# Mixture of experts: gate and up products in one PSUM bank, the down product behind the next expert's first products

## What is computed

```python
for e in range(N_EXPERTS):                       # 16; two of them count for each row
    he = jax.nn.silu(h2 @ w_gate[e]) * (h2 @ w_up[e])          # 1024 -> 256
    moe = moe + combine[..., e:e + 1] * (he @ w_down[e])       # 256 -> 1024
x = x + moe
y = rmsnorm(x, g_final)
```

## Time and profile before

| | before |
|---|---|
| median of 3 runs (lowest to highest) | 462.22 us (460.56 to 463.78) |
| profiled execution: its time, its span | 466.0 us, 464.2 us |
| PE busy | 431.6 us, 93% of the span |
| DVE, ACT, POOL busy | 229.3, 150.2, 108.9 us |
| chain that ended last | PE 78%, DVE 8%, ACT 4%, issue 3%, DMA 2%, POOL 2% |
| two of its lines | gate and up (L1120) 25%, down (L1128) 12% |
| DMA queues: q1 (SP), q0 (POOL) | 71.97 MB, 18.96 MB |

### The profile page before, as it was taken

How to read it: one execution, slowest core, us unless ns; L and a number is a source line. 1 busy time by engine, 2 the same in 40 slices (tenths; PEclk the granted TensorE clock), 3 DMA queues, 4 the chain that set the end, 5 groups by cost and what they waited for, 6 DMA issues and landing times.

```text
span 464.2 us, 7463 instructions
## 1 busy us (share of the span) xinstructions
PE 431.6 (93%) x2858; PEld 351.0 (76%) x2858; DVE 229.3 (49%) x590; ACT 150.2 (32%) x397; POOL 108.9 (23%) x200
## 2 busy tenths in 40 slices
PE   7899999999999998999987899999999999999970
PEld 3786999988867766888763888888877777778850
DVE  3854233536688985443338462222455555544441
ACT  5474223425567663321113210112222211222240
POOL 2011002000342341310003022222443333333221
PEclk9999999999999999999999999999999999999995
DMA  7851607124000299132215999998999988952110
GB/s 269 286 151 48 214 1 229 55 74 118 1 3 0 95 419 388 75 140 91 92 56 209 367 368 363 342 356 343 341 353 340 325 322 327 339 185 61 50 59 20
DMA packets 32072, 91.38 MB, mean 197 GB/s; under 512 B 11193, under 2 KB 11705, under 8 KB 27942
## 3 DMA queue, kind: packets, MB, share of 16 engines
q1 hardware_dynamic: 20790, 71.97, 42.2%
q0 software_dynamic: 11248, 18.96, 11.5%
HBM read 86.38 MB, written 26.01 MB: 242 GB/s over the span
## 4 chain that ended last, share of the span: by engine, by line
PE 78%; DVE 8%; ACT 4%; issue 3%; DMA 2%; POOL 2%; POOLq 0%; SPq 0%; DVEq 0%; ACTq 0%
PE ps L1120 25%; PE ps L1128 12%; PE ps L774 10%; PE ps L776 9%; PE ps L775 9%; PE ps L1070 2%; PE ps L1113 2%; PE ps L895 2%; PE ps L930 2%; DMA region_x<-in_x_prompt 1%; PE ps L913 1%; PE ps L1057 1%; DMA region_x<-h_rows,idx 1%; PE ps L770 1%; DVE region_t L1980 1%
## 5 line engine op out<-in xcount | busy, mean ns | idle before, releaser
L1120 PE MATMUL ps<-region_p,region_a 128*128 128x128 f32 x512 | 59.0, 276 | 0.0
L1120 PEld LDWEIGHTS ps<-region_p,region_a 128*128 128x128 f32 x512 | 57.9, 192 | 0.5 <-issue 0.5
L776 PE MATMUL ps<-region_a_r,region_w_r 128*128 128x288 f32 x192 | 56.5, 294 | 0.0
L1980 DVE TENSOR_TENSOR region_t<-region_t,ps 128x256 f32<-128x256 f32 x16 | 6.7, 422 | 84.2 <-PE ps L1120 84.2
L774 PE MATMUL ps<-region_a_r,ring_r 128*128 128x288 f32 x128 | 40.5, 317 | 0.0
L1470 ACT ACTIVATE region_t<-ps 128x256 f32<-128x256 f32 x16 | 6.1, 384 | 100.7 <-PE ps L1120 93.9
L775 PE MATMUL ps<-region_a_r,ring_r 128*128 128x288 f32 x128 | 37.7, 295 | 0.0
L776 PEld LDWEIGHTS ps<-region_a_r,region_w_r 128*128 128x128 f32 x192 | 36.0, 188 | 0.0
L1460 ACT ACTIVATE region_p<-ps,gffn_sb 128x128 f32<-128x128 f32 x64 | 18.3, 368 | 52.9 <-PE ps L1113 52.9
L1128 PE MATMUL ps<-region_a,region_t 128*128 128x512 f32 x64 | 29.2, 599 | 2.3 <-DVE region_t L1980 2.3
L775 PE MATMUL ps<-region_w_r,mix_r 128*128 128x512 f32 (+1 forms) x80 | 31.3, 391 | 0.0
(11 more groups left out here) (305 smaller groups left out, 903.4 us busy)
## 6 DMA issues: line engine op xcount, KB each, us to landing
region_a<-in_w_gate SPq DMA_DIRECT2D x8, 1024.0 KB
region_a<-in_w_up SPq DMA_DIRECT2D x8, 1024.0 KB
region_a<-in_w_down SPq DMA_DIRECT2D x8, 1024.0 KB
region_w<-in_w_in SPq DMA_DIRECT2D x2, 2048.0 KB, 10.7
region_w<-in_w_out SPq DMA_DIRECT2D x2, 2048.0 KB, 7.9
ring<-in_w_gate SPq DMA_DIRECT2D x4, 1024.0 KB
ring<-in_w_up SPq DMA_DIRECT2D x4, 1024.0 KB
ring<-in_w_down SPq DMA_DIRECT2D x4, 1024.0 KB
```

The source lines that it names most:

```text
L776: return pe.matmul(out, lhs_lo, rhs_hi, start=False, stop=last)
L1120: ins = pe.matmul(ps[:, bank, c * P:(c + 1) * P], w[:, k, c * P:(c + 1) * P], xT[:, b, k, :], start=(k == 0), stop=(k == KC - 1))
L1980: dve.tensor_tensor(heT[:, i % 2], gact[:, i % 2], ps[:, 3, 0:FE].rearrange("p (c s) -> p c s", c=FC), ALU.mult).then_inc(he_ready, 1)
```

## The change

Gate and up of one expert now share a PSUM bank (gate in its first half, up in its second), and experts alternate between banks 2 and 3. One semaphore, `up_full`, stands for both, and SiLU waits for it; `gate_full` is gone. On PE the down product of expert i-1 stands behind gate, up and row transposes of expert i. Lists 2, 3 and 4 are made together behind the first down product. The down product of expert 14 follows that of expert 13 in banks of its own (6 and 7), and that of expert 15 stands at the end as before. SP's loads of down weights, POOL's stores and gathers of the sums, and the adds, square sums and finishes on DVE and ACT each move one expert later with it. The overflow count on DVE moves ahead of lists 2 and 3 and of the first add. `store_acc` and `store_out` are queued one expert later, and the number of transfers stays the same.

The core of the diff (semaphore declaration and overflow path left out, empty lines too):

```diff
@@ -530,12 +529,14 @@
             for i in range(E - RING):
                 sp.wait_ge(up_full, i + 1)
                 load_gate_up(i % RING, expert_at(i + RING))
-                sp.wait_ge(down_done, 2 * i + 2)
-                load_down(i % RING, expert_at(i + RING))
+                if i >= 1:
+                    sp.wait_ge(down_done, 2 * i)
+                    load_down((i - 1) % RING, expert_at(i - 1 + RING))
                 if i == 1:
                     sp.wait_ge(routed, 1)
                     sp.dma_start(gfin, g_final.rearrange("(a d) -> a d", a=1).to_broadcast([P, D])).then_inc(gfin_loaded, 16)
+            sp.wait_ge(down_done, 2 * (E - RING))
+            load_down(RING - 1, expert_at(E - 1))
             sp.wait_ge(down_done, 2 * E)
             n_ov = sp.value_load(ctl[0:1, MAXOV:MAXOV + 1], min_val=0, max_val=MAXOV)
@@ -702,19 +703,19 @@
                 if i == 1:
                     gather_acc(0)
                     gather_acc(1)
-            for i in range(E - 1):
-                if i > RING:
-                    pool.wait_ge(final_ready, i - RING)
-                    store_out(i - 1, out_stored[(i - 1) % 2])
+            for i in range(E):
+                if i > RING + 1:
+                    pool.wait_ge(final_ready, i - 1 - RING)
+                    store_out(i - 2, out_stored[i % 2])
                 if i + EARLY < E:
                     gather_h2(i + EARLY)
-                if i < E - RING:
-                    if i == 0:
+                if 1 <= i <= E - RING:
+                    if i == 1:
                         pool.wait_ge(idx_ready, EARLY + 1)
-                    pool.wait_ge(added, i + 1)
-                    store_acc(i, acc_stored[i % 2])
-                if i + 2 < E:
-                    gather_acc(i + 2)
+                    pool.wait_ge(added, i)
+                    store_acc(i - 1, acc_stored[(i - 1) % 2])
+                if 1 <= i < E - 1:
+                    gather_acc(i + 1)
             pool.wait_ge(routed, 1)
             n_ov = pool.value_load(ctl[0:1, MAXOV:MAXOV + 1], min_val=0, max_val=MAXOV)
@@ -1113,19 +1114,18 @@
                     ins = pe.transpose(ps[:, k // 4, (k % 4) * P:(k % 4 + 1) * P], src[:, k, :], ident[:, :])
                 ins.then_inc(signal, 1)
-            def gate_up(slot, b, gate_signal, up_signal):
-                for w, bank, signal in ((wg_sb[slot], 2, gate_signal), (wu_sb[slot], 3, up_signal)):
+            def gate_up(slot, b, signal):
+                for w, first in ((wg_sb[slot], 0), (wu_sb[slot], FC)):
                     for c in range(FC):
                         for k in range(KC):
-                            ins = pe.matmul(ps[:, bank, c * P:(c + 1) * P], w[:, k, c * P:(c + 1) * P],
+                            ins = pe.matmul(ps[:, 2 + b, (first + c) * P:(first + c + 1) * P], w[:, k, c * P:(c + 1) * P],
                                             xT[:, b, k, :], start=(k == 0), stop=(k == KC - 1))
-                    if signal is not None:
-                        ins.then_inc(signal, 1)
-            def down(slot, b, signal):
+                ins.then_inc(signal, 1)
+            def down(slot, b, signal, bank=4):
                 for half in range(2):
                     for c in range(FC):
-                        ins = pe.matmul(ps[:, 4 + half, :], heT[:, b, c, :], wd_sb[slot][:, c, half * 512:(half + 1) * 512],
+                        ins = pe.matmul(ps[:, bank + half, :], heT[:, b, c, :], wd_sb[slot][:, c, half * 512:(half + 1) * 512],
                                         start=(c == 0), stop=(c == FC - 1))
                     if signal is down_done or half == 1:
                         ins.then_inc(signal, 1)
@@ -1153,7 +1153,7 @@
                 pe.wait_ge(xT_dve, i + 1)
                 pe.wait_ge(xT_act, i + 1)
                 pe.wait_ge(ring_loaded[u], it * 48 + 48)
-                gate_up(u, b, gate_full, up_full)
+                gate_up(u, b, up_full)
                 if first:
                     pe.wait_ge(tab_ready, 1)
                     for n in range(2):
@@ -1161,14 +1161,24 @@
                 if left is None or left >= 1:
                     pe.wait_ge(xg_loaded[1 - b], it * (8 * RING) + 16 * ((u + 1) // 2 + 1))
                     transpose_rows(1 - b, xg_transposed)
-                pe.wait_ge(he_ready, i + 1)
-                if not first:
-                    pe.wait_ge(added, i)
-                down(u, b, down_done)
-                if first:
-                    lists_of(2)
-                if left is None or left >= EARLY:
+                if not first and left != 0:
+                    pe.wait_ge(he_ready, i)
+                    if not (isinstance(it, int) and i == 1):
+                        pe.wait_ge(added, i - 1)
+                    down((u - 1) % RING, 1 - b, down_done, 4)
+                if isinstance(it, int) and i == 1:
+                    for n in (1, 2):
+                        lists_of(n)
+                if not first and (left is None or left >= EARLY):
                     lists_of(EARLY)
+                if left == 1:
+                    pe.wait_ge(idx_ready, E + EARLY)
+                    pe.wait_ge(he_ready, i + 1)
+                    down(u, b, down_done, 6)
+                if left == 0:
+                    pe.wait_ge(he_ready, E)
+                    pe.wait_ge(added, E - 2)
+                    down(u, b, down_done, 4)
             for u in range(RING):
                 expert(0, u, None)
@@ -1466,8 +1476,8 @@
             ins.then_inc(xT_act, 1)
             def silu(i):
-                act.wait_ge(gate_full, i + 1)
-                act.activation(gact[:, i % 2], ps[:, 2, 0:FE].rearrange("p (c s) -> p c s", c=FC),
+                act.wait_ge(up_full, i + 1)
+                act.activation(gact[:, i % 2], ps[:, 2 + i % 2, 0:FE].rearrange("p (c s) -> p c s", c=FC),
                                ACT.Silu).then_inc(gact_ready, 1)
             def square_sum(i):
@@ -1479,9 +1489,12 @@
                                accum_out=ssq[:, i % 2:i % 2 + 1]).then_inc(squared, 1)
             for i in range(E):
+                if i == E - 1:
+                    square_sum(E - 3)
+                    square_sum(E - 2)
                 silu(i)
-                if i > RING:
-                    square_sum(i - 1)
+                if RING + 1 < i < E - 1:
+                    square_sum(i - 2)
                 if i + 1 < E:
                     act.wait_ge(xg_transposed, i + 2)
                     for k in range(4, KC):
@@ -1978,15 +1991,15 @@
                 dve.wait_ge(gact_ready, i + 1)
                 dve.wait_ge(up_full, i + 1)
                 dve.tensor_tensor(heT[:, i % 2], gact[:, i % 2],
-                                  ps[:, 3, 0:FE].rearrange("p (c s) -> p c s", c=FC), ALU.mult).then_inc(he_ready, 1)
-            def add_rows(i):
+                                  ps[:, 2 + i % 2, FE:2 * FE].rearrange("p (c s) -> p c s", c=FC), ALU.mult).then_inc(he_ready, 1)
+            def add_rows(i, bank=4):
                 q, w = i % RING, i % LISTS
                 acc = xacc[:, q, :].rearrange("p (b d) -> p b d", b=2)
                 dve.wait_ge(down_done, 2 * i + 2)
                 dve.wait_ge(xacc_loaded[q], 16 * (i // RING + 1))
-                dve.scalar_tensor_tensor(acc, ps[:, 4:6, :], slot_w[:, w:w + 1], acc, ALU.mult, ALU.add).then_inc(added, 1)
+                dve.scalar_tensor_tensor(acc, ps[:, bank:bank + 2, :], slot_w[:, w:w + 1], acc, ALU.mult, ALU.add).then_inc(added, 1)
             def inverse_root(i, do):
@@ -2002,6 +2015,12 @@
             def finish(i, signal):
                 dve.scalar_tensor_tensor(yf[:, i % 2, :], xacc[:, i % RING, :], root[:, 3:4], gfin,
                                          ALU.mult, ALU.mult).then_inc(signal, 1)
+            def finish_row(i):
+                dve.wait_ge(squared, i - RING + 1)
+                inverse_root(i, step)
+                dve.wait_ge(gfin_loaded, 16)
+                finish(i, final_ready)
             for i in range(E - 1):
                 he_out(i)
@@ -2012,19 +2031,20 @@
                 rows_out((i + 1) % 2).then_inc(xT_dve, 1)
                 if i >= 1 and i + EARLY < E:
                     expert_onehot(i + EARLY)
-                if i > RING:
-                    dve.wait_ge(squared, i - RING)
-                    inverse_root(i - 1, step)
-                    dve.wait_ge(gfin_loaded, 16)
-                    finish(i - 1, final_ready)
-                if i == 0:
+                if i == 1:
                     lists_out(2)
-                if i + EARLY < E:
-                    lists_out(i + EARLY)
-                add_rows(i)
+                    lists_out(3)
+                if i > RING + 1:
+                    finish_row(i - 2)
+                if i >= 1:
+                    add_rows(i - 1)
+                    if i + EARLY < E:
+                        lists_out(i + EARLY)
                 if i == 0:
                     count_overflow()
```

(6 more changed lines are left out.)

1 line of the change is left out of this document (removed).

## The result

The changed kernel takes **465.74 us** (median of 8 runs, 463.81 to 467.81), the kernel before 462.27 (8 runs, 460.34 to 463.87): a ratio of 1.008, 95% interval 1.0054 to 1.0106. So it is 3.5 us slower, where 3.9 us less were forecast, and it lies above the range.

A forecast was written before the change was run, and what follows sets the result against it. TensorE, busy 93% of the span, was taken as the bound, so only its standing time could be won. Terms: -5.6 - 0.7 + 1.3 + 0.45 + 0.2 + 0.4 = -3.9 us, giving 458.3 us, range 456.4 to 462.4.

The forecast's parts named there:

- Experts 6 to 12: Deferred down product covers late news of up (1 to 1.4 us); seven periods fall from 12.479 to 11.675: -5.6 us.
- Rival 2: PE itself is held, a stall that stays wherever the down product stands; 1.7 us slower, 463.9 us; chance 0.09.
- marks near 12.4: Sign of rival 2: starts of row transposes in experts 6 to 12 stay about 12.4 us apart without a wait.
- Third gather: Expert 3's rows, gathered only after list 3 is read, may land late behind SP's weights: +0.2 us, bounds 0 and 2.0.
- rival 4: More than forecast: lists and gather cost nothing, xT pause 1.14; gain 4.9, 457.3 us; chance 0.07.
- Expert 1: Its heT no longer waits behind the overflow count on DVE; period 12.34, 0.66 over, shortens: -0.7 us.
- Start: Before expert 1's gate nothing covers the evacuation of its transposes into xT, so PE stands: +1.3 us.
- Lists: At expert 1, list 4 waits until DVE has read list 2's bank: +0.45 us, bounds 0 and 0.6.
- SiLU at the end: Expert 15's uncovered heT is released by SiLU behind up instead of by up itself: +0.4 us.
- Clock: TensorE's granted clock was 1.00 in both stretches looked at, one holding PE waits; nothing charged.
- rival 1: DMA becomes the bound, period about 12.0: 460.4 us; a late third gather (2.0) gives the same; chance 0.20.
- rival 3: Slower: gathers behind output stores take over 14.9 us from issue to landing; at 16.4, about 468.8 us; chance 0.08.

The follow-up runs named there:

- b_count: Kernel before with only the overflow count moved, behind expert 0's xT and ahead of lists 2 and 3 and the first add; 461.34 us, ratio 0.9966.
- e_lists_sep: Changed kernel with lists 2 and 3 behind expert 1's transposes, gate and up in separate banks, SiLU behind gate; 462.51 us, ratio 1.0011 to the kernel before.
- a_again: The changed kernel, unchanged, in a second profiled execution; 467.41 us (4 runs), ratio 1.0113 to the kernel before.
- b_again2: The kernel before, unchanged, profiled again (third profiled execution); 462.47 us.
- b_again4: The kernel before, unchanged, profiled again (fifth profiled execution); 462.40 us.

## Why the prediction was wrong

**Experts 6 to 12, -5.6: this step failed.** It priced the change by the periods of one profiled execution, and the loss belonged to that execution. The period did go to 11.67, but it was 11.67 in typical executions of the kernel before. The hint stood in the prediction's own text: the profiled execution took 466.0 us, 3.8 above the median, and I carried the -3.9 over to the median instead of asking whether the 3.8 were the same microseconds. With this term at nothing the prediction's own sum is 1.7 us slower, not 3.9 faster. Rival 2 says so (463.9), but by another mechanism, a stall of PE itself that stays in the changed kernel; its sign, marks near 12.4, did not come. What the lag was in the first execution stays open. The prediction took from the earlier trace rows that the transposes behind up were done on time. That holds for experts 7 to 12; at expert 6 ACT, which waits for these transposes, is late too, 1.48 us behind the mark of the earlier trace rows instead of 1.08:

```profile
337.29 1.14 ACT L1460 ACTIVATE region_p<-ps,gffn_sb 128x128 f32<-128x128 f32 x4 [3.44 <-PE ps L1113]
```

So a stall of PE itself is not ruled out there.

**Third gather, +0.2: mis-sized.** It measured 1.86 and 1.53. The bounds of 0 and 2.0 were right and I chose near the lower one, though the row nearest to it, today's third gather behind the same SP queue, was the upper. Counted from the first transposes (254.94 before, 256.95 after), the issue came when forecast (24.95 us, forecast 25.06) and PE wanted the rows when forecast (32.1, forecast 32.0). The landing was at 33.96, the upper bound's 288.8 is 33.86, and the +0.2 stands for 32.2. (288.8 less 286.9 is 1.9, which the prediction gives as 2.0; and by its own terms rival 4 is 4.8 us, not 4.9.)

**Expert 1, -0.7: right,** by b_count (12.34 to 11.67). **Start, +1.3: right** (1.28). **Lists, +0.45: close** (0.35). **SiLU at the end, +0.4: right** (0.38, and e_lists_sep gives it back). **Clock, nothing charged:** a_again has no fall behind the wait and the first execution has one of 1.8 us; falls of this size come and go in all kernels (below), so the term stays at nothing for the mean difference, as far as these runs tell: the mean granted clock is 0.982 in the 8 runs of the changed kernel and in the 69 of the kernel before (0.978 in the four of a_again).

The sum with the measured terms is -0.7 + 1.3 + 0.35 + 1.5 to 1.9 + 0.4 = 2.9 to 3.3 us slower. The stretches say 3.5: a_again without its fall of the clock, 208.70 - 1.63 = 207.07, against 205.23 - 1.64 = 203.6 of b_again2. The times say 3.5 (8 runs; 5.2 in the four of a_again). With a_again's own 1.53 for the gather the sum is 2.9, so 0.6 is left over. Restarts of PE behind its waits may hold a part (in b_again4 the period that ends with the wait of 0.89 is 1.17 over); that is not shown. Of rival 1 the second half came, the late third gather; its bound by DMA did not, nor did rival 3: no period of experts 4 to 13 is above 11.68 in the seven profiled executions with the deferred down product. Rival 4 did not come: list 4 and the gather both cost.

## What to carry to other kernels

Before a wait is priced from a profile, compare the profiled execution with the median: an excess as large as the wait is a reason to look at a second execution first. A change that takes away all the waits it aimed at, and shows it in the profile, proves nothing about the time if the waits weren't in the usual run. And when a step is moved, the transfer that hangs on it moves too: here a list made 9.5 us later (270.36 - 254.94 = 15.4 us behind the first transposes before, 25.0 after) put a gather behind 1.5 MB of SP's transfers, and that cost more than the stall that was real.

## What the runs showed of the hardware

The granted clock falls for some microseconds in code that is the same in all kernels, at the same places but only in some executions: at 178 to 182.5 us in 4 of the 14 profiled ones (0.62 to 0.69, the others 1.00), in expert 0 in 7 of the 14 (0.85 to 0.87, and 11.5 to 11.6 us from the first to the second transposes, instead of the 9.9 to 10.0 of the five others with the same order). In all 14 PE stands 1.3 to 1.4 us ahead of expert 0's gate product, so the wait alone does not make the fall. The windows (PE, PEld, DVE, ACT, POOL busy, granted clock, DMA share, GB/s) of the changed kernel:

```profile
178.00:182.50 4.50, 4.50 (x14) 3.51 (x13) 1.93 (x3) 0.78 (x2) 0.00 (x0) 0.62 1.00 410
...
290.90:297.20 6.30, 6.25 (x22) 3.68 (x22) 1.42 (x2) 1.14 (x4) 0.00 (x0) 0.73 0.91 370
```

of the kernel before in the first of these stretches:

```profile
178.00:182.50 4.50, 4.50 (x21) 3.61 (x20) 1.88 (x4) 1.49 (x2) 0.00 (x0) 1.00 1.00 412
```

and of b_again2 from its first to its second transposes:

```profile
255.40:267.20 11.80, 10.39 (x83) 10.24 (x84) 3.76 (x14) 1.53 (x5) 1.69 (x2) 0.86 0.89 336
```

At 178 to 182.5 us no instruction was changed; the changed kernel had 0.62 there, between the two levels 0.5 (1.2 GHz) and 1.00 (2.4 GHz), with PE busy all through, and lost 1.6 us (by the starts of the same products in both traces); the kernel before had 1.00. In both PE had stood 1.5 us just ahead of the stretch, up to 176.66 and 176.29. b_again2 had 0.86 in expert 0 and lost 1.6 us. Behind the wait of 1.86 us for the third gather the clock fell (0.73), behind that of 1.53 in a_again it did not (1.00 from 291.5 to 296.5). These falls of 1.5 to 1.8 us are half of the whole effect, so one execution against another does not tell it; stretches have to be compared mark by mark.
